# A mixture-of-experts kernel whose first block of transposed rows is formed from the rows in SBUF by products with a slot matrix

## The reference

```python
h2 = rms_norm(x, g_norm2[l]) * (1.0 + sc2) + sh2
ffn = hier_moe(h2, w_group[l], b_group[l], w_router[l], b_router[l], ...)
x = x + gt2 * ffn
```

## Time and profile before

| what | value |
|---|---|
| median of 3 executions | 1888.47 us (1886.64 to 1890.67) |
| the profiled execution's own time | 1894.03 us |
| its span | 1892.1 us |
| mean granted TensorE clock | 0.944 of full |
| PE busy | 1728.9 us (91%) |
| VectorE busy | 1209.2 us (64%) |
| ScalarE busy | 485.4 us (26%) |
| GpSimd busy | 681.8 us (36%) |
| DMA | 230.52 MB, mean 122 GB/s |

### The profile page before, as it was taken

The page is one execution under the profiler, slowest core; times in us unless marked ns, Lnnn a source line. Parts: engine busy times, 40 slices in busy tenths (PEclk is TensorE's granted clock), DMA queues, the critical chain, the costliest instruction groups (busy, mean ns, idle before and its releaser), DMA issues.

```text
span 1892.1 us, 29374 instructions
## 1 busy us (share of the span) xinstructions
PE 1728.9 (91%) x11994; PEld 1332.4 (70%) x11994; DVE 1209.2 (64%) x1607; ACT 485.4 (26%) x731; POOL 681.8 (36%) x383
## 2 busy tenths in 40 slices
PE   5999888888879999999879999999898995999998
PEld 4888557776757777777758788777676873666665
DVE  6959556663558888888768159386444525566674
ACT  3121424532021001010141122221241004444442
POOL 2666000001326666666436534345234651000000
PEclk8999859998889999999989999999898997999999
DMA  5232331131124222222223212113121343688884
GB/s 210 90 107 94 112 112 48 48 100 61 45 90 166 90 90 89 89 89 89 89 71 105 92 45 68 67 45 125 49 67 45 102 187 145 247 352 325 325 346 159
DMA packets 34069, 230.52 MB, mean 122 GB/s; under 512 B 4132, under 2 KB 4388, under 8 KB 8232
## 3 DMA queue, kind: packets, MB, share of 16 engines
q1 hardware_dynamic: 30240, 214.48, 31.2%
q10 hardware_dynamic: 2136, 10.24, 1.4%
q0 software_dynamic: 1584, 4.21, 0.7%
HBM read 220.98 MB, written 9.50 MB: 122 GB/s over the span
## 4 chain that ended last, share of the span: by engine, by line
PE 76%; DVE 13%; ACT 4%; DMA 3%; issue 3%; POOL 0%; SPq 0%; DVEq 0%; ACTq 0%; POOLq 0%
PE psum L391 75%; DVE arena L1576 4%; DVE arena L1582 4%; DMA arena<-units 2%; ACT arena L1203 2%; PE psum L395 1%; DVE arena L1579 1%; ACT L1203 1%; DVE expert_lo L1576 1%; DMA normed<-units 1%; ACT expert_hi L1203 1%; DVE residual L1576 0%; DMA arena<-x 0%; POOL slots L2462 0%; ACT tiny L1203 0%
## 5 line engine op out<-in xcount | busy, mean ns | idle before, releaser
L1203 ACT ACTIVATE arena<-psum 128x512 f32<-128x512 f32 (+4 forms) x295 | 149.1, 520 | 894.3 <-PE psum L391 781.9
L391 PE MATMUL psum<-arena 64*64 64x64 f32 (+6 forms) x2756 | 219.1, 268 | 34.8 <-DVE arena L1576 19.6
L391 PE MATMUL psum<-normed_hi,w_in_hi 128*128 128x512 f32 x512 | 205.5, 401 | 6.0 <-DVE in_lo L1576 3.4
L391 PEld LDWEIGHTS psum<-arena 64*64 64x64 f32 (+4 forms) x2756 | 144.9, 152 | 92.6 <-issue 47.5
L391 PE MATMUL psum<-normed_hi,w_in_lo 128*128 128x512 f32 x512 | 203.1, 397 | 0.0
L391 PE MATMUL psum<-in_lo,w_in_hi 128*128 128x512 f32 x512 | 201.7, 394 | 0.0
L1582 DVE SCALAR_TENSOR_TENSOR arena<-arena,fixed_data 128x512 f32<-128x512 f32 x134 | 187.8, 1401 | 13.5 <-DVE arena L1579 0.2
L1576 DVE TENSOR_TENSOR arena<-arena,psum 128x512 f32<-128x512 f32 (+2 forms) x200 | 110.7, 589 | 118.2 <-PE psum L391 71.6
L2419 POOL TENSOR_TENSOR w_ff_lo<-weight_ring,w_ff_hi 128x1024 fp32r<-128x1024 f32 x66 | 167.2, 2533 | 5.5
L2419 POOL TENSOR_TENSOR w_in_lo<-weight_ring,w_in_hi 128x1024 fp32r<-128x1024 f32 x64 | 163.6, 2557 | 5.3
L2417 POOL TENSOR_SCALAR w_in_hi<-weight_ring 128x1024 fp32r<-128x1024 f32 x64 | 72.7, 1136 | 215.2 <-PE psum L391 185.7
(11 more groups left out here) (243 smaller groups left out, 3657.4 us busy)
## 6 DMA issues: line engine op xcount, KB each, us to landing
weight_ring<-units SPq DMA_DIRECT2D x124, 1024.0 KB, 4.8
arena<-units SPq DMA_DIRECT2D x55, 1024.0 KB, 7.8
normed<-units SPq DMA_DIRECT2D x20, 1024.0 KB, 8.2
slots<-arena ACTq DMA_DIRECT2D x7, 516.0 KB, 9.2
arena<-slots SPq DMA_DIRECT2D x7, 516.0 KB, 5.8
fixed_data<-fixed ACTq DMA_DIRECT2D x1, 2944.0 KB, 12.0
arena<-x SPq DMA_DIRECT2D x4, 512.0 KB, 6.0
arena<-bias_rows ACTq DMA_DIRECT2D x2, 896.0 KB, 5.6
```

The costliest lines, as they stand in the source:

```text
L391: return nc.tensor.matmul(o, l, r, start=start, stop=stop)
L1203: return nc.scalar.activation(o, i, func, **kw)
```

## The change

For block 0 the transposed, scaled rows are formed on PE from `x_rows`, which stay in SBUF, and not from the rows that came back from DRAM. Four matrices `hot[t]` (token by slot) hold the token's norm factor where its slot matches the column and zero elsewhere; VectorE makes them after `rank`, from a row of numbers 0 to 127 that GpSimd writes (`slot_ids_i`) and VectorE turns to float (`slot_ids`). `first_rows` adds up four products for each of the eight feature tiles. Block 0's split rows lie in `fixed_data` in place of constants that are no longer read, since the old place overlaps `x_rows`. On VectorE, `split_rows(0)` comes before the `groups_ready` operations and `expert_lo(1)`, and the wait for the loaded rows of block 0 stands just before step 0. The trip through DRAM itself stays, since `xb[0]` is still needed. Blocks 1 to 6 are as before.

```diff
+        fix_at = nc.sbuf_base
         fix = ctx.enter_context(nc.sbuf_tensor("fixed_data", [P, N_FIX], F32))
...
-        xt_hi = [part(f"rows_hi{i}", 12288 + 2048 * i, D) for i in range(2)]
-        xt_lo = [part(f"rows_lo{i}", 12288 + 2048 * i + D, D) for i in range(2)]
-        xt_raw = [A(12288 + 2048 * i + D, D) for i in range(2)]
+        sel_at = C0 + CONSTS["sel16"][0]
+        xt_at = [(sel_at, fix_at), (12288, None), (14336, None)]
+        xt_hi = [part(f"rows_hi{i}", o, D, at_) for i, (o, at_) in enumerate(xt_at)]
+        xt_lo = [part(f"rows_lo{i}", o + D, D, at_) for i, (o, at_) in enumerate(xt_at)]
+        xt_raw = [fix[:, sel_at + D:sel_at + 2 * D], A(12288 + D, D), A(14336 + D, D)]
+        slot_ids_i, slot_ids = A(16416, P).bitcast(I32), A(16416 + P, P)
+        hot = [A(16896 + t * P, P) for t in range(NT)]
+        def xt_of(b):
+            return 1 + b % 2 if b else 0
...
+            def first_rows():
+                for j in range(8):
+                    emptied(pe, "x_rows", j)
+                pe.wait_ge(sem("hot_ready"), NT)
+                for i in range(2):
+                    o = open_("rows", i, 4 + i)
+                    for k in range(4):
+                        for t in range(NT):
+                            last = mm(o[:, k * P:(k + 1) * P], x_rows[:, t, (4 * i + k) * P:(4 * i + k + 1) * P], hot[t],
+                                      t == 0, t == NT - 1)
+                    close(last, "rows", i)
             def rows_in(b):
-                pe.wait_ge(sem("scale_ready"), b + 1)
+                pe.wait_ge(sem("scale_ready"), b)
...
-            rows_in(0)
+            first_rows()
...
+            dve.wait_ge(sem("slot_ids_made"), 1)
+            link(V.tensor_copy(slot_ids, slot_ids_i))
             filled(dve, "route_t")
...
             link(V.tensor_reduce(rank, grid, AX.X, ALU.add))
+            for t in range(NT):
+                ts(hot[t], slot_ids, rank[:, t:t + 1], rs4[:, t:t + 1], ALU.is_equal, ALU.mult).then_inc(sem("hot_ready"), 1)
             link(V.tensor_copy(slot, rank))
...
             expert_lo(0)
-            expert_lo(1)
+            split_rows(0)
             g3 = gid_m.rearrange("p (j c) -> p j c", c=3)
...
             V.tensor_copy(gid_i, gid_f).then_inc(sem("groups_ready"), 1)
-            scale_of(0)
-            split_rows(0)
+            expert_lo(1)
+            dve.wait_ge(sem("rows0_loaded"), 16)
             for s in range(NX):
...
             split_units(w_br[2], 6 + 4)
+            filled(pool, "mix2", KT - 1)
+            nc.gpsimd.iota(slot_ids_i, [[1, P]], base=0, channel_multiplier=0).then_inc(sem("slot_ids_made"), 1)
             pool.wait_ge(sem("slots_ready"), 1)
```

More of the change, by code:

```diff
@@ L1158, in expert_up @@
                     c = slice(k * P, (k + 1) * P)
-                    mm(o, xt_hi[b % 2][:, c], hi[:, :, :, k, :], k == 0, False)
-                    mm(o, xt_hi[b % 2][:, c], lo[:, :, :, k, :], False, False)
-                    last = mm(o, xt_lo[b % 2][:, c], hi[:, :, :, k, :], False, k == KT - 1)
+                    mm(o, xt_hi[xt_of(b)][:, c], hi[:, :, :, k, :], k == 0, False)
+                    mm(o, xt_hi[xt_of(b)][:, c], lo[:, :, :, k, :], False, False)
+                    last = mm(o, xt_lo[xt_of(b)][:, c], hi[:, :, :, k, :], False, k == KT - 1)
                 close(last, "expert_up", s)
@@ L1549, in rows_hi @@
                     emptied(act, "rows", 2 * b + i)
-                    f(xt_hi[b % 2][:, c], xt_raw[b % 2][:, c], ACT.Copy).then_inc(sem("rows_hi"), 1)
+                    f(xt_hi[xt_of(b)][:, c], xt_raw[xt_of(b)][:, c], ACT.Copy).then_inc(sem("rows_hi"), 1)
             for s in range(2):
@@ L2341, in split_rows @@
                     for k in range(4 * i, 4 * i + 4):
-                        last = ts(xt_raw[b % 2][:, k * P:(k + 1) * P], PSB[4 + i][:, k % 4 * P:(k % 4 + 1) * P],
+                        last = ts(xt_raw[xt_of(b)][:, k * P:(k + 1) * P], PSB[4 + i][:, k % 4 * P:(k % 4 + 1) * P],
                                   gm2[:, k:k + 1], mod[:, 24 + k:25 + k], ALU.mult, ALU.add)
@@ L2347, in split_rows @@
                     dve.wait_ge(sem("rows_hi"), 2 * b + i + 1)
-                    tt(xt_lo[b % 2][:, c], xt_raw[b % 2][:, c], xt_hi[b % 2][:, c].bitcast(F32), ALU.subtract)\
+                    tt(xt_lo[xt_of(b)][:, c], xt_raw[xt_of(b)][:, c], xt_hi[xt_of(b)][:, c].bitcast(F32), ALU.subtract)\
                         .then_inc(sem("rows_split"), 1)
```

## The result

| what | before | after |
|---|---|---|
| median | 1890.74 us (20 executions, 1886.64 to 1897.10) | 1879.54 us (20 executions, 1869.78 to 1889.85) |
| span of the profiled execution | 1892.1 us | 1874.9 us |
| its mean granted clock | 0.944 | 0.951 |

The ratio of after to before is 0.9943, with a 95% interval of 0.9930 to 0.9957: 11 us faster, where 12.35 were forecast. The span of the one profiled execution fell by 17.2 us, more than the medians: the execution profiled before took 3.3 us more than the median of its 20, the one profiled after 2.8 us less. So each stretch has to be looked at by itself, from an event that both kernels have: VectorE's addition of the last `mix2` tile, at 1569.38 before and at 1568.03 after.

A forecast was written before the change was run, and what follows sets the result against it. PE was taken to wait before step 0 for the rows' trip through DRAM. Step 0 at 1584.62 + 1.1 + 4.40 + 4.22 = 1594.35 against 1606.70, so 1888.47 − 12.35 = 1876.1 us; range 1872.5 to 1882.

The forecast's parts named there:

- What bound the kernel: End of second layer: PE stands idle before step 0, waiting behind the rows' 15.03 us trip through DRAM.
- The time itself: Whole kernel: step 0 and all behind it 12.35 us earlier, median 1876.1 us; chance 0.70.
- Slot numbers and `hot`: GpSimd iota 0.5 us and conversion at most 0.28, cost nothing; VectorE's four `hot` operations 1.1 us on the path.
- PE's products: `first_rows` on PE: 32 products from 1584.05, done at 1591.1, hidden behind `expert_lo(0)` with 0.4 us to spare.
- VectorE's order: `expert_lo(0)` ends at 1590.1, `split_rows(0)` follows; step 0 4.22 us later at 1594.35, not 1606.70.
- Clock: Step 0 on PE: same slow start as before; rival, full clock from its start, 1.1 us more, 1875.0, chance 0.08.
- The rows' arrival: Before `e_act(0)`: rows at 1601.1, 1.1 us spare; rival, slower scatters make it bind, 1878 if 3 us more, chance 0.09.
- The register reads: SyncE's nine reads before `load_up(3)`: taken as 0 loss; rival, they bind, 7.3 us lost, 1883.4, chance 0.07.
- The weight stream: Rival, expert steps behind step 0: transfers that start no earlier take the gain back; half lost is 1882.3, chance 0.04.
- a lasting low clock: Rival, PE behind step 0: clock stays low, slower than before; 1909.7 with seven steps slow, chance 0.02.
- Its signs of being wrong: Profile after: DMA-ended idle before `e_act(0)`, late `load_up(3)`, late iota, products outlasting `expert_lo(0)`, or PE waits clearly above 5.1 us.

The follow-up runs named there:

- again: The changed kernel measured once more, nothing edited: 1883.02 us, ratio 0.9947 to the kernel before.
- lo_first: Changed kernel with `expert_lo(1)` put back ahead of `split_rows(0)`: 1884.59 us, ratio 0.9957 to the kernel before.
- order_only: Kernel before, with only `expert_lo(1)` moved behind `split_rows(0)`; block 0 still from the gathered rows: 1891.97 us, ratio 0.9990.
- half: Changed kernel with half the tokens' rows left out of `first_rows`, 32 instructions and not 64: 1879.78 us, ratio 0.9941 to the kernel before.
- best: Changed kernel with filler products in PE's holes, each `hot` matrix waited for by itself, and register reads behind `load_down(3)`: 1878.39 us, ratio 0.9928.
- double: Changed kernel with each product of `first_rows` issued twice, 128 instructions and not 64: 1890.99 us, ratio 0.9994 to the kernel before.
- before_again: Kernel before, unedited, one execution for a second profile: step 0 at 37.58 us, `e_act(0)` at 45.44, 274.5 from there to the end; no median.
- again_2: Changed kernel, unedited, one execution for a third profile: step 0 at 26.73 us, `e_act(0)` at 33.16, 279.6 to the end; no median.
- reads_late: Changed kernel with SyncE's nine register reads moved behind `load_up(3)` and `load_down(3)`: 1881.14 us, ratio 0.9940 to the kernel before.
- early: Changed kernel with `first_rows` waiting for each `hot` matrix by itself, not for all four: 1883.41 us, ratio 0.9944 to the kernel before.

## Why the prediction was right, and which term was off

- **What bound the kernel:** right. Step 0 waited for the rows' trip; taking it off this path moved step 0 by 10.6 us and `e_act(0)` by 12.0 in the first pair of profiles. Over two profiles before and three after, `e_act(0)` stands at 45.3 and 33.9 us, 11.4 apart, and the medians of 20 executions are 11.2 apart. The gain is made in this stretch; nothing behind it was shown to add or to take.
- **The time itself:** 1879.54 us is 3.4 above the 1876.1 of the forecast. 2.3 of them are the start of the sum: the median before was 1888.47 in three executions and 1890.74 in twenty. The other 1.1 are the gain, 11.2 and not 12.35, and the profiles agree: `e_act(0)` at 33.9 on average, where 32.8 were forecast.
- **Slot numbers and `hot`:** right. The iota took 0.23 us, the conversion 0.23 in VectorE's wait, the four operations 1.12 us together in the row (1.1 predicted).
- **PE's products, "Cost nothing, hidden behind `expert_lo(0)`, with 0.4 us to spare":** this is the term that was wrong. The work was taken at half its size. The prediction counted "32 products where `rows_in(0)` issued 16" and priced 16 by the row with x16. But `rows_in(0)` is 2 × 4 = 8 products in the code, and its row counts 16 because a float32 product is two instructions in the trace. (The "16 products" of `rows_in` in the description ahead of the prediction are instructions too; the 24 of `expert_up`, in the short format, are 24 in both counts.) `first_rows` has 2 × 4 × 4 = 32 products and so 64 instructions: 9.0 to 10.0 us instead of 3.9 to 7.0. The excess over the cover put step 0 at 26.7 to 27.7 us and not at 24.97, a loss of 1.7 to 2.7.
- **VectorE's order:** right to 0.2 us. With half the products, and again with fillers and an early start, step 0 stood at 24.74 and 24.75.
- **Clock:** the same slow start as before was expected. In two of the three profiles of the changed kernel step 0 ran at the full clock from its first product to its last. This gave 1.4 us back there, and so most of the error above was covered: 33.1 us to `e_act(0)` against the 32.8 predicted. That is luck: two errors of opposite sign. Where the clock did not help, in `again`, `e_act(0)` was at 35.4. No run shows that the change itself raises the clock in step 0.
- **The rows' arrival:** did not bind; VectorE's wait before `e_act(0)` is put down to ScalarE. The rival feared scatters that run slower beside `split_rows(0)`. They ran faster, and the loads were issued at 26.9 us behind the last `mix2` addition, where 1.1 later than before would have been 28.5.
- **The register reads:** hidden, but dearer than taken. From the end of the row loads' issue, 1594.96 + 2.07 = 1597.03, to `load_up(3)` at 1602.25 they are 5.2 us, 0.58 each, where 3.8 in all were assumed. The lateness, 1.6 us, lay within the 6.1 us of slack that the prediction counted; no run tested the slack. The Trainium skill, "Runtime: NRT & Kernel Launch", section "Instruction fetch mechanics", has about 200 ns per register, from HBM; these reads, from SBUF and with what stands between them, took almost three times that.
- **The weight stream and a lasting low clock:** neither came. The third stretch is not longer after the change, and in windows after from 1601 to 1830 the clock is 1.00 (0.98 in the last 45 us).
- **Its signs of being wrong:** two of them showed, the products not done when `expert_lo(0)` ended and `load_up(3)` behind step 0's end. They point at the two terms above. PE's waits in the expert steps were 2.5 us after, but 6.7 and 7.6 in the two other profiles of the same kernel, so this sign could not have told anything.

## What to carry to other kernels

Before a group of products is priced by a row, divide the row's count by the products in the code: float32 ones count double here, and an error of two in the work is easily made when the old and the new loop are compared. When a transfer is taken off the path, work out the next two candidates to the microsecond; here PE and VectorE were 2 us apart, and halving or doubling the work of one told in two runs which of them was the path. Where single spans of one kernel differ by more than the effect, count from a common event ahead of the change to one behind it.

## What the runs showed of the hardware

- A GpSimd scatter of 128 rows took 1.9 us beside `expert_lo(1)`, a VectorE subtraction with both inputs in SBUF, and 0.95 us beside VectorE work that reads PSUM or beside none, four ways round: before and `lo_first` 1.9, after and `order_only` 0.95. The time does not simply follow the overlap: the fourth scatter of `lo_first`, from 1587.53 to 1589.42, met `expert_lo(1)` only until 1588.6. A fourth scatter that lay beside `rows_lo`, also such a subtraction, for nearly all of its time took 1.59 us in `half` and in `best`. Timelines of GpSimd and VectorE in `half`:

```profile
1590.85 1.59 POOL L2491 DMA_INDIRECT slots<-arena  x1 [0.30 <-issue]
```

```profile
1590.94 1.47 DVE L1599 TENSOR_TENSOR rows_lo<-fixed_data,rows_hi 128x512 fp32r<-128x512 f32 x2
```

  The Trainium skill, "SBUF — State Buffer", section "Who interferes with whom", says that such a `tensor_tensor` contends with GpSimd's reads, and infers that descriptor generation, which it says needs the write interface, is spared. These runs agree with the first. Which part of a scatter grew the trace does not show, so they speak against the second only if it was the generation of its descriptors.
- Short scatters do not by themselves make the trip short: in `double` they took 0.95 us too, and from the first scatter to the row loads it was 11.90 us (1585.49 to 1597.39), where it was 10.3 after. Why was not looked into.
- PE's clock fell at the start of `first_rows`, after holes of 3.96 and 1.99 us in which it was still granted in full, and held where the hole was 0.42 us, in one profile. The same kernel had it fall 5 us earlier in another execution (`again`). Nor does the hole ahead of step 0 decide by itself how step 0 starts: behind the same 2.85 us its first product took 0.50 us, at the full clock, in four profiles (`before_again`, after, `again_2`, `reads_late`) and 0.71 to 0.80 in five (before, `again`, `double`, `early`, `order_only`). Step 0's 24 products took from 5.9 to 8.6 us.
- The expert steps behind `e_act(0)` varied from 273.6 to 279.9 us between executions. PE's waits for VectorE's tensor-tensor operations went with it in the main, from 1.3 us (273.6) over 2.5 (273.7), 5.1 (277.5) and 6.7 (278.7) to 7.6 (279.6), less so in `best` (2.9 at 276.8) and `order_only` (6.1 at 279.9). ScalarE's waits for weight loads into `arena` go the same way: 18.4 and 17.1 us in the two shortest, 24.4 and 23.8 in `again` and `again_2`. Why the loads come late in one execution and not in another was not looked into.
